# Moving the causal mask to TensorE and two small steps to ScalarE in a fused attention, mLSTM and expert-retrieval block

## What is computed

```python
xn = rmsnorm(x)
proj = xn @ w_in                    # q, k, v (8 heads x 64); q, k, v, o, i, f (4 heads x 128); gates
# stick-breaking attention, for each 128-query block
z = q @ k.T * 64 ** -0.5            # causal: s < t, strictly
sp = where(causal, softplus(z), 0)
w = where(causal, exp(log_sigmoid(z) - reverse_cumsum(sp_next)), 0)
y_sb = w @ v
# mLSTM
qk = silu(causal_conv(ml_qk, width 4) + b)
y_ml = o * headnorm(mlstm(q_m, k_m, v_m, i, f))   # decayed sums over chunks
h = x + (sigmoid(g_sb) * (y_sb @ W_sb) + sigmoid(g_ml) * (y_ml @ W_ml)) @ w_out
# PEER: 8 heads, 2 x 128 keys, top 16 -> 128 experts for each token
a = gate * gelu(sum(u[idx] * hn))   # u and v: 16384 x 1024 each
out = rmsnorm(h + sum(a * v[idx]))
```

## Time and profile before

| what | value |
|---|---|
| median of 3 runs | 3404.8 us (3401.5 to 3405.33) |
| the profiled execution, its own time | 3402.06 us |
| its span, first to last instruction | 3399.9 us |
| instructions | 40366 |
| mean granted TensorE clock, 1 is full | 0.891 |
| DMA, mean over the span | 377 GB/s |
| the indirect gathers | 1073.81 MB of 1280.41 MB |
| VectorE busy | 2138.2 us, of it 1244.3 us in the dot products (line 1498) |

### The profile page before, as it was taken

The page is one execution under the profiler, slowest core; times in us unless marked ns, Lnnn a source line. Parts: engine busy times, 40 slices in busy tenths (PEclk is TensorE's granted clock), DMA queues, the critical chain, the costliest instruction groups (busy, mean ns, idle before and its releaser), DMA issues.

```text
span 3399.9 us, 40366 instructions
## 1 busy us (share of the span) xinstructions
PE 2636.4 (78%) x14560; PEld 1342.2 (39%) x14560; DVE 2138.2 (63%) x4956; ACT 1078.5 (32%) x3394; POOL 1198.7 (35%) x1049
## 2 busy tenths in 40 slices
PE   7998887998888778988788778888787555555555
PEld 5776634554454244544354234444253111111111
DVE  1322579775457886775456797776447755775444
ACT  3111443332323543332223363332322232222222
POOL 0000333333333443433333353333334444444443
PEclk8999998999999899999898899999998777777787
DMA  3345998999999999999999989999999999999997
GB/s 112 111 124 191 404 401 314 385 417 417 417 415 416 388 361 417 419 418 417 418 414 409 384 350 397 418 419 416 415 415 416 418 400 420 421 420 410 421 421 319
DMA packets 225670, 1280.41 MB, mean 377 GB/s; under 512 B 25152, under 2 KB 25152, under 8 KB 94400
## 3 DMA queue, kind: packets, MB, share of 16 engines
q0 software_dynamic: 147456, 1073.81, 77.0%
q1 hardware_dynamic: 63104, 162.09, 13.1%
q10 hardware_dynamic: 14912, 41.95, 3.2%
HBM read 1260.97 MB, written 16.78 MB: 376 GB/s over the span
## 4 chain that ended last, share of the span: by engine, by line
DMA 39%; PE 34%; DVE 12%; ACT 6%; issue 5%; POOL 3%; ACTq 0%; POOLq 0%; DVEq 0%
DMA rowsb<-uv,e_idx 38%; PE yacc L758 13%; PE mixp L496 9%; DVE rowsb L1498 5%; POOL rowsb L824 3%; PE mixp L521 3%; PE mixp L508 2%; DVE area L1171 2%; PE mixp L534 2%; ACT diag L1093 2%; ACT wg L1088 2%; PE mixp L545 1%; DVE area L1202 1%; ACT area L842 1%; ACT gmt L1078 1%
## 5 line engine op out<-in xcount | busy, mean ns | idle before, releaser
L824 POOL DMA_INDIRECT rowsb<-uv,e_idx x1024 | 1194.0, 1166 | 2171.6 <-PE yacc L758 1673.0
L1498 DVE CUSTOM_DVE_ANT_0 rowsb<-rowsb,hnrow 128x1024 f32<-128x1024 f32 x1024 | 1244.3, 1224 | 886.0 <-DMA rowsb<-uv,e_idx 883.2
L758 PE MATMUL yacc<-rowsb,diag 64*64 64x512 f32 x8192 | 1233.9, 727 | 685.0 <-ACT diag L1093 668.9
L758 PEld LDWEIGHTS yacc<-rowsb,diag 64*64 64x64 f32 x8192 | 301.7, 152 | 1435.7 <-ACT diag L1093 997.7
L1078 ACT ACTIVATE gmt<-dots 128x2 f32<-128x2 f32 x512 | 104.1, 203 | 1779.1 <-DVE dots L1498 1778.6
L496 PE MATMUL mixp<-area,wt 128*128 128x256 f32 x2304 | 535.9, 387 | 7.1 <-ACT area L842 5.9
L496 PEld LDWEIGHTS mixp<-area,wt 128*128 128x128 f32 x2304 | 432.6, 192 | 145.4 <-issue 90.8
L1093 ACT ACTIVATE diag<-ident,wg 128x64 f32<-128x64 f32 x1024 | 300.3, 340 | 16.7
L842 ACT ACTIVATE area<-mixp 128x512 f32<-128x512 f32 (+3 forms) x384 | 162.6, 467 | 308.8 <-PE mixp L496 163.1
L1088 ACT ACTIVATE wg<-gmt,gate 128x1 f32<-128x1 f32 x1024 | 245.5, 286 | 17.4
L521 PE MATMUL mixp<-area,wt 128*128 128x256 f32 x1024 | 241.8, 392 | 9.5 <-DMA wt<-w_query_ 8.3
(11 more groups left out here) (185 smaller groups left out, 1668.0 us busy)
## 6 DMA issues: line engine op xcount, KB each, us to landing
wt<-w_merge SPq DMA_DIRECT2D x96, 512.0 KB, 8.1
wt<-w_feat SPq DMA_DIRECT2D x80, 512.0 KB, 8.0
wt<-w_query_ SPq DMA_DIRECT2D x64, 512.0 KB, 12.0
wt<-w_tok SPq DMA_DIRECT2D x32, 512.0 KB, 11.1
wt<-w_out_ SPq DMA_DIRECT2D x32, 512.0 KB, 8.0
rowsb<-uv,e_idx POOLq DMA_INDIRECT x1024, 13.7
area<-x_rows ACTq DMA_DIRECT2D x4, 1024.0 KB, 12.5
area<-keysT ACTq DMA_DIRECT2D x16, 256.0 KB, 12.1
```

The lines of the kernel that those rows point to most:

```text
L758: last = pe.matmul(yacc[at:at + HP, r, c * NCH:(c + 1) * NCH], diag[r * HP:(r + 1) * HP, s, :], rowsb[r * HP:(r + 1) * HP, s, D + c * NCH: ...
L824: pool.indirect_dma_start(rowsb[:, n % RS, :], None, uv, bass.IndirectOffsetOnAxis(ap=e_idx[:, i % 2, k:k + 1], axis=0)).then_inc(row_load ...
L1498: dve.tensor_tensor_reduce(rowsb[:, s, 0:D], rowsb[:, s, 0:D], hnrow[:, i % 2, :], 1.0, 0.0, ALU.mult, ALU.add, dots[:, s:s + 1]).then_inc ...
```

## The change

Three edits. (1) `tri` now holds -1e30 where the key isn't before the query and 0 elsewhere. In `logits`, for the group that holds the query's own tile, TensorE adds `ident` times `tri` onto the last 128 columns of the logits in PSUM, for each of the two heads, and signals after it. Tanh of such a logit is -1, so r is 1. VectorE's maximum goes; in its place the scan waits until the subtraction before it has ended. (2) The tap of lag 0 is a ScalarE ACTIVATE (Identity with scale and bias from `vec`) from PSUM, one step after TensorE's product; the rest of `conv` and both steps of silu come one step later than before. (3) In step s = 1 of an mLSTM head ScalarE makes `vw` right after the Exp, by four ACTIVATEs, after TensorE has used the `vw` of the head before; VectorE waits for it before it changes `ex`.

```diff
@@ logits, TensorE
-                            pe.matmul(X[:, h, 0:n], sbq[own, hp, il * P:(il + 1) * P],
-                                      keys_sb[own, hp, g * NCH:g * NCH + n], start=True, stop=True).then_inc(x_done[h], 1)
+                            own_tile = g == (t0 + il) // 4
+                            last = pe.matmul(X[:, h, 0:n], sbq[own, hp, il * P:(il + 1) * P],
+                                             keys_sb[own, hp, g * NCH:g * NCH + n], start=True, stop=not own_tile)
+                            if own_tile:
+                                last = pe.matmul(X[:, h, n - P:n], ident[:, :], tri[:, :], start=False, stop=True)
+                            last.then_inc(x_done[h], 1)
@@ constants, GpSimd
-                set_(pool.memset(tri[:, :], 1.0))
+                set_(pool.memset(tri[:, :], -BIG))
@@ PROJ2 steps, ScalarE
-                        if 3 <= k < 3 + N_CONV:
-                            n = k - 3
+                        if 2 <= k < 2 + N_CONV:
+                            n = k - 2
+                            key = ("mlqk", b, n)
+                            at = V_CONV + n * (CONV + 1) + CONV - 1
+                            ready(act, key)
+                            act.activation((mlq if n < 4 else mlk)[:, n % 4, :], X[:, bank(key), 0:N], ACT.Identity,
+                                           scale=vec[:, at:at + 1], bias=vec[:, at + 1:at + 2]).then_inc(tap_ready, 1)
+                        if 4 <= k < 4 + N_CONV:
+                            n = k - 4
                             act.wait_ge(conv_done, b * N_CONV + n + 1)
@@ mix steps, ScalarE
                             act.activation(ex[:, 0:NEX], ex[:, 0:NEX], ACT.Exp, scale=-1.0).then_inc(ex_ready, 1)
+                            if b < NB - 1:
+                                act.wait_ge(ex_ready, b * ML_HEADS + h + 1)
+                                if h > 0:
+                                    ready(act, ("kc", b, h - 1))
+                                elif b > 0:
+                                    ready(act, ("kc", b - 1, ML_HEADS - 1))
+                                for t, at in enumerate((N - 1, NEX - 1)):
+                                    act.activation(vw[:, t, 0:ML_DIM], mlv[:, t, h * P:(h + 1) * P], ACT.Copy, scale=ex[:, at:at + 1])
+                                    ins = act.activation(vw[:, t, ML_DIM:ML_DIM + 1], ex[:, at:at + 1], ACT.Copy)
+                                ins.then_inc(vw_ready, 1)
@@ scan, VectorE
                         dve.wait_ge(rem_ready, before + 2 * g_ * (v + 1))
-                        mark(dve.tensor_tensor(r_[:, m - P:m], r_[:, m - P:m], tri[:, :], ALU.max))
-                        settle()
+                        scanned = 2 * (NV * b + v) + h
+                        if scanned > 0:
+                            dve.wait_ge(wts_ready, scanned)
@@ conv, VectorE
                         ready(dve, key)
-                        mark(dve.tensor_scalar(dst, pk[:, 0:N], tap(CONV - 1), tap(CONV), ALU.mult, ALU.add))
+                        dve.wait_ge(tap_ready, b * N_CONV + n + 1)
                         for lag in range(CONV - 1, 0, -1):
-                            settle()
+                            if lag < CONV - 1:
+                                settle()
@@ PROJ2 steps, VectorE
-                        if 2 <= k < 2 + N_CONV:
-                            conv(k - 2)
-                        if 4 <= k < 4 + N_CONV:
-                            n = k - 4
+                        if 3 <= k < 3 + N_CONV:
+                            conv(k - 3)
+                        if 5 <= k < 5 + N_CONV:
+                            n = k - 5
@@ mix steps, VectorE
                             if b < NB - 1:
-                                for t, at in enumerate((N - 1, NEX - 1)):
-                                    dve.tensor_scalar(vw[:, t, 0:ML_DIM], mlv[:, t, h * P:(h + 1) * P],
-                                                      ex[:, at:at + 1], None, ALU.mult)
-                                    mark(dve.tensor_copy(vw[:, t, ML_DIM:ML_DIM + 1], ex[:, at:at + 1]))
-                                settle()
+                                dve.wait_ge(vw_ready, b * ML_HEADS + h + 1)
```

More of the change, by code:

```diff
@@ L202, in build @@
             "neg_ready", "ln_ready", "m_ready", "em_ready", "exp_step"))
-        conv_done, silu_th, qk_ready = sem("conv_done"), sem("silu_th"), sem("qk_ready")
+        tap_ready, conv_done, silu_th, qk_ready = sem("tap_ready"), sem("conv_done"), sem("silu_th"), sem("qk_ready")
         ex_ready, vw_ready, c_ready = sem("ex_ready"), sem("vw_ready"), sem("c_ready")
```

## The result

The changed kernel takes 3407.4 us (median of 15 runs, 3402.9 to 3415.6) against 3402.7 us of the kernel before on the same chips (15 runs, 3396.6 to 3409.1). The ratio is 1.0016, with a 95% interval of 1.001 to 1.0022: about 5 us slower, inside the 0.2% that I had set as "no change", but outside zero.

A forecast was written before the change was run, and what follows sets the result against it. Bounds: the head before the gathers and four VectorE-bound stretches in blocks 1 to 3; elsewhere gathers fill DMA. Terms 8.2 - 4.4 - 3.0 + 0.5 = +1.3 us gave 3403.4, with 2.7 for the median 3406; range 3392 to 3418.

The forecast's parts named there:

- Head, +8.2 us: Block 0's stick-breaking stage: mask matmuls delay the gathers; six tenths weight on the lower clock, four tenths on the upper.
- The term for the lower level, +14.4: Block 0's stage if TensorE stays at 1.2 GHz: mask streaming, lost overlap of heads and form changes add 14.4 us.
- The second rival: Head's stage stays at the lower clock, late masks save nothing: +11.9 us, 3417; chance 0.32. Also called "TensorE takes over".
- The other end, -1.1: Block 0's stage if the added matmuls bring TensorE's clock to 2.4 GHz: 1.1 us shorter.
- Late stages, -4.4 us: Stick-breaking of blocks 1 to 3: removed maxima gain nothing in block 1, 60% of 3.1 + 4.2 us in the others.
- The end of 10.7 us: Stick-breaking of blocks 1 to 3: the most that removing VectorE's maxima could save, 20.5 x 0.52 us.
- Taps, -3.0 us: Block 1's eight convolutions: first taps taken from VectorE save 3.0 us; elsewhere hidden or worth 0.
- the end of 4.6: Block 1's convolutions: the most the taps could save, with the wait between first and second tap.
- Decayed values, +0.5 us: mLSTM heads of blocks 0 to 2: VectorE waits for ScalarE's four instructions, mostly hidden; +0.5 us, ends 0 and 4.
- the rival of the tables: Identity needs its own table: two loads a tap delay block 1's diagonals, perhaps +8 us, 3414; chance 0.04.
- VectorE stays the only bound: Clock rises in the head, late stages and convolutions pay in full: -16.4 us, 3388; chance 0.21.
- TensorE takes over: Serial logits and masks cost +14.4 us in the head and cancel the late stages' saving: +11.9 us, 3417; chance 0.32.

The follow-up runs named there:

- late_mask: The whole change, but block 0 keeps VectorE's maximum and has no mask matmuls; ratio 0.9970 to the kernel before.
- masks_after_both: The whole change, but both heads' logits are issued first and both masks after them; ratio to the kernel before 0.9963, in a repeat 0.9966.
- tap_and_vw: Edits 2 and 3 alone (taps and decayed values on ScalarE), the mask's maximum back on VectorE; ratio 0.9985 to the kernel before.
- zeros_in_block0: The kernel before with nothing removed; in block 0 TensorE adds zeros to each head's logits, behind both logits; ratio 1.0005 to the kernel before.

## Why the prediction held, and which of its terms did not

*The whole.* I forecast 3406 and no change; the ratio says +5.4 us on an own time of 3402, near 3407. The sum was +1.3. That the forecast held is in part luck. By the ratios the steps are -5.1 for taps and decayed values together, -5.1 for the late masks and +15.6 for the masks in the head (from late_mask's 0.9970 to 1.0016). The head's term was 7 us too small, and nearly half of that was made up by the taps and late masks, which gave more than their terms. With its own value for the lower level, which is what was measured, the sum would have been +7.5 us, more than the 6.8 that I called no change. And the 1.4 us between 3406 and 3407.4 are nearer than the sum was, since the median of before came out 2.1 us lower here than in the three runs that I started from.

*Head, +8.2 us: right mechanism, mis-sized by the choice of clock.* The term for the lower level, +14.4, measured 14.6 us (89.56 to 104.17), piece by piece as worked out: lost overlap, two changes of form (a query of 128 keys 2.0 us where I had 1.9, one of 256 keys 2.4 for 2.3, flips included). What failed is the step "I take six tenths at the lower level". In the changed kernel the stage ran at 0.50 throughout, in spite of the longer runs of matmuls. The second rival had this right. The other end, -1.1, needed the clock, and it was seen only in another order: masks_after_both at 0.99, its stage 2.6 us shorter than before (86.92 for 89.56).

*Late stages, -4.4 us: right in size, the mechanism seen in part.* Late_mask against tap_and_vw gives 5, the stages' own lengths 3.3; neither is clear of its scatter. The first of the three windows was to gain nothing because TensorE takes over. On the average block 1's stage did gain only 0.3 us, and 19.97 of 20 us and a chain of TensorE alone show why in one stretch. But late_mask, with the same code there, took 63.2 us for that stage and the changed kernel 66.4, so one execution doesn't settle it. In block 2, where I expected 60% of 3.1 us, nothing was gained; block 3 gained 2.9 for 60% of 4.2. The end of 10.7 us may have been too small: with no mask at all the kernel is 13 us faster than with the maxima, of which at most 0.5 is the head's, but the intervals reach down to 4. What lies behind the difference wasn't tested.

*Taps, -3.0 us: right place, probably too small.* They gave 5.4 (0.9984), above the end of 4.6, but the interval runs from 2.4 to 8.2 us and holds both. The stretch from block 1's gate rows to block 2's first scan is 7 us shorter on the average with the taps away (593.3 for 600.6), which speaks for too small. I multiplied eight instructions and took seven tenths, because VectorE was busy for only 91%. The order may help too: the gate rows no longer stand behind the first convolution. Which of the two gave how much stays open, since both are in edit 2.

*Decayed values, +0.5 us: right.* 1.0000 by itself, good to 3 us, as expected of work under cover of saturated gathers and TensorE's projections; the cover itself wasn't tested.

*No table loads.* The lines of Identity (972) and of the copies (1016, 1017) on ScalarE stand without a load of their own:

```profile
L972 ACT ACTIVATE area<-mixp,vec 128x256 f32<-128x256 f32 x32 | 17.7, 554 | 23.3 <-PE mixp L496 21.9 <-issue 1.3
...
L1016 ACT ACTIVATE area<-area 128x128 f32<-128x128 f32 x24 | 9.5, 395 | 0.4
L1017 ACT ACTIVATE area<-area 128x1 f32<-128x1 f32 x24 | 4.5, 187 | 0.0
```

So the rival of the tables falls. The Trainium skill, "ScalarE: Activation LUTs", Table sets, lists identity and copy among the functions of every set, and the trace agrees: the changed kernel has 104 table loads, as many as before. The tap costs 0.554 us and not the 0.47 that I took from line 896: it has two operands from memory, scale and bias, where that has one. The Trainium skill, "ScalarE: Activation LUTs", What ACT_TABLE_LOAD costs, gives 186 ns + 0.833 ns for each column and 93 for each such operand, by which I estimate 585 ns; the trace has 554. It changes nothing here.

*The two rivals.* "VectorE stays the only bound" is refuted for the change as made, but masks_after_both comes near its gain (12.6 of 16.4 us). "TensorE takes over" is right for the head, and for some 8 of the 13 us that the maxima cost. It had the late masks at nothing and the taps at -3.0; with 5 us from each its +11.9 came out at +5.4.

## What to carry to other kernels

Before work is moved to an engine that looks free, look at what its instructions overlap with there: a matmul over the full height of the array between two that run side by side on its halves costs here its own streaming, the overlap of its neighbours, and a change of form on each side. In a query that came to two and a half to three times its own price (2.2 and 2.6 us for 0.86). Issue such matmuls behind the group and not inside it; that one change of order turned a kernel 0.16% slower into one 0.37% faster. And ask for every moved instruction in which stage it stands: the masks lost more in the head (15.6 us) than they won later (5), and the taps won only around one block's convolutions.

## What the runs showed of the hardware that I had not expected

The form change is regular: with logits and masks alternating each piece of 128 columns took 0.72 us at the lower clock, 0.29 beyond its streaming, and the flips after a mask 0.23 us and not 0.42. By the Trainium skill, "TensorEngine Tiling (Array Packing)", Key Properties, a change of the tiling mode drains the engine; the trace agrees, with that 0.29 us for each change beyond the streaming.

The clock of the head's stage is not fixed by the program. Two executions of one kernel showed 0.99 and 0.72 in the same window, and zeros_in_block0 had a spread of 20 us in its times. All kernels without masks in block 0 showed 0.50 to 0.53 there, and so did the two with masks in between; only the two with full-height matmuls behind both logits there rose (0.99 and 0.72 in masks_after_both, 0.62 in zeros_in_block0). Why the alternating order, in which TensorE was busy for 20.4 of 22 us, did not, stays open.
